# Dilated attention: two heads of a tile together, in rounds of blocks, each head in its own score bank

## What is computed

```
s = jnp.einsum('bnqrhd,bnkrhd->bnrhqk', qb, kc) * (Dh ** -0.5)
s = jnp.where(mask[None, :, None, None], s, NEG_BIG_2)
m = jnp.max(s, axis=-1, keepdims=True)
p = jnp.exp(s - m)
den = jnp.sum(p, axis=-1, keepdims=True)
o = jnp.einsum('bnrhqk,bnkrhd->bnqrhd', (p / den), vc)
lse = (m + jnp.log(den))[..., 0]
```

## Time and profile before

| | us |
|---|---|
| median of 3 runs | 3933.51 |
| profiled execution | 3931.43 |
| its span | 3930.1 |
| PE busy | 3568.4 |
| DVE busy | 1358.0 |
| POOL busy | 1278.8 |
| ACT busy | 1130.7 |

### The profile page before, as it was taken

How to read it: one execution, slowest core, us unless ns; L and a number is a source line. 1 busy time by engine, 2 the same in 40 slices (tenths; PEclk the granted TensorE clock), 3 DMA queues, 4 the chain that set the end, 5 groups by cost and what they waited for, 6 DMA issues and landing times.

```text
span 3930.1 us, 37316 instructions
## 1 busy us (share of the span) xinstructions
PE 3568.4 (91%) x15666; PEld 2807.9 (71%) x15666; DVE 1358.0 (35%) x2169; ACT 1130.7 (29%) x1545; POOL 1278.8 (33%) x335
## 2 busy tenths in 40 slices
PE   6887899998967999999996799989999889969998
PEld 5654588886734788888875688868888666647887
DVE  4337541323166422221228521242212332463123
ACT  2234332322144322322222322222222222223222
POOL 4210044442200344444433444444444420014442
PEclk9987799999977999999998899999999987769999
DMA  3110023332200233333331233324333220012332
GB/s 114 60 50 1 22 91 103 93 90 65 65 18 1 75 97 97 97 89 94 102 91 54 65 95 99 91 91 145 102 97 93 79 89 27 1 38 77 95 101 71
DMA packets 462184, 296.78 MB, mean 76 GB/s; under 512 B 14330, under 2 KB 454192, under 8 KB 462016
## 3 DMA queue, kind: packets, MB, share of 16 engines
q1 hardware_dynamic: 453664, 277.09, 24.3%
q10 hardware_dynamic: 8352, 17.30, 1.3%
HBM read 285.97 MB, written 8.39 MB: 75 GB/s over the span
## 4 chain that ended last, share of the span: by engine, by line
PE 82%; DVE 13%; ACT 3%; issue 1%; POOL 0%; DMA 0%; SPq 0%; ACTq 0%; DVEq 0%
PE bank L472 23%; PE bank L473 23%; PE bank L474 23%; PE bank L313 12%; DVE ta L733 1%; DVE xl L745 1%; DVE x L735 1%; DVE ta L1107 1%; DVE ta L512 1%; PE bank L1858 0%; POOL wlo L412 0%; DVE u L1391 0%; DVE scr L1632 0%; DVE ta L1888 0%; DVE tiny L1380 0%
## 5 line engine op out<-in xcount | busy, mean ns | idle before, releaser
L412 POOL TENSOR_TENSOR wlo<-raw,whi 128x2048 fp32r<-128x2048 f32 (+3 forms) x288 | 1210.3, 4203 | 2514.2 <-ACT whi L405 2514.2
L472 PE MATMUL bank<-xh,whi 128*128 128x512 f32 x2432 | 976.2, 401 | 70.1 <-DVE xl L745 54.4
L473 PE MATMUL bank<-xl,whi 128*128 128x512 f32 x2432 | 960.7, 395 | 0.0
L474 PE MATMUL bank<-xh,wlo 128*128 128x512 f32 x2432 | 960.4, 395 | 0.0
L405 ACT ACTIVATE whi<-raw 128x2048 fp32r<-128x2048 f32 (+3 forms) x288 | 503.4, 1748 | 712.3 <-PE bank L474 677.3
L472 PEld LDWEIGHTS bank<-xh,whi 128*128 128x128 f32 x2432 | 465.6, 191 | 198.7 <-DVE xl L745 49.3
L474 PEld LDWEIGHTS bank<-xh,wlo 128*128 128x128 f32 x2432 | 464.8, 191 | 99.6
L473 PEld LDWEIGHTS bank<-xl,whi 128*128 128x128 f32 x2432 | 465.7, 191 | 93.0
L472 PE MATMUL bank<-ah,whi 128*128 128x512 f32 x1216 | 473.0, 389 | 0.0
L473 PE MATMUL bank<-al,whi 128*128 128x512 f32 x1216 | 473.0, 389 | 0.0
L474 PE MATMUL bank<-ah,wlo 128*128 128x512 f32 x1216 | 473.0, 389 | 0.0
(11 more groups left out here) (333 smaller groups left out, 3331.6 us busy)
## 6 DMA issues: line engine op xcount, KB each, us to landing
raw<-in_ffn_w_gate SPq DMA_DIRECT2D x88, 512.0 KB, 4.0
raw<-in_ffn_w_up SPq DMA_DIRECT2D x88, 512.0 KB, 5.2
raw<-in_w_up SPq DMA_DIRECT2D x64, 512.0 KB, 4.8
raw<-in_w_down SPq DMA_DIRECT2D x64, 512.0 KB, 4.9
raw<-in_w_in SPq DMA_DIRECT2D x56, 512.0 KB, 4.7
raw<-in_ffn_w_down SPq DMA_DIRECT2D x64, 384.0 KB, 3.9
raw<-in_ffn_w_down SPq DMA_DIRECT2D x64, 320.0 KB, 3.5
raw<-in_w_out SPq DMA_DIRECT2D x16, 512.0 KB, 4.0
```

The costliest lines, as they stand in the source:

```text
L412: g.e.tensor_tensor(self.wlo[slot][:, 0:n], self.raw[slot][:, 0:n], self.whi[slot][:, 0:n].bitcast(F32), ALU.subtract).then_inc(self.lo_ma ...
L472: pe.e.matmul(bank, hi[:, at:at + P], xh, start=k == ks[0], stop=False)
L473: pe.e.matmul(bank, hi[:, at:at + P], xl, start=False, stop=False)
L474: last = pe.e.matmul(bank, lo[:, at:at + P], xh, start=False, stop=k == ks[-1])
```

## The change

PE, DVE and ACT take both heads of a tile in each step. `pairs(g)` with its places in two banks is replaced by `rounds(g)`: group 0 has two rounds, of three and of four pairs, groups 1 and 2 have one of four. In a round head 0 uses the first score bank and head 1 the second. PE issues all score products of the round, heads alternating, and then all masks, heads alternating. Head 0's weights are transposed into the transpose bank, head 1's into its own score bank after its exps. The output products of a round alternate between the heads as well; in group 0 those of the first round stand behind the scores of the second. There are 8 `yield`s to an item in groups 1 and 2, and 13 in group 0.

```diff
--- before.py
+++ after.py
@@ -1778,23 +1778,12 @@
             return self.ta[1][:], self.tb[1][:], spare(10), [wide(self.spare[:, k:k + 2, :]) for k in (11, 13)], (4, 5, 6, 7), stats
         return self.ta[0][:], self.tb[0][:], s(8), [wide(self.scr[:, k:k + 2, :]) for k in (0, 2)], (0, 1, 2, 3), stats
 
-    def pairs(self, g):
-
-        if g == 0:
-            pairs = [(0, 0, CAUSAL)] + [x for b in range(1, NB) for x in ((b, b - 1, PAST), (b, b, CAUSAL))]
-        else:
-            pairs = [(b, b, CAUSAL if g == 1 else CAUSAL4) for b in range(NB)]
-        spots, col = [], 0
-        for n in range(len(pairs)):
-            if g == 0 and n == 3:
-                col = T
-            spots.append((col // T, col % T))
-            col += P
-        spans = []
-        for qb in range(NB):
-            mine = [n for n in range(len(pairs)) if pairs[n][0] == qb]
-            spans.append((*spots[mine[0]], P * len(mine)))
-        return pairs, spots, spans
+    def rounds(self, g):
+
+        if g:
+            return [([(b, b, CAUSAL if g == 1 else CAUSAL4) for b in range(NB)], [(b, b * P, P) for b in range(NB)])]
+        meet = lambda b: [(b, b - 1, PAST), (b, b, CAUSAL)]
+        return [([(0, 0, CAUSAL)] + meet(1), [(0, 0, P), (1, P, 2 * P)]), (meet(2) + meet(3), [(2, 0, 2 * P), (3, 2 * P, 2 * P)])]
 
     def dilated_block(self, g):
         return (lambda t, b: t[:, b * P:b * P + P]) if g == 0 else (lambda t, b: t[:, b::4])
@@ -1813,9 +1802,9 @@
                 yield
             q, k, val = [self.qkv[:, 12 * m + 4 * g + i, :] for m in range(3)]
             block = self.dilated_block(g)
-            pairs, spots, spans = self.pairs(g)
+            rounds = self.rounds(g)
             if old:
-                pe.wait_ge(a, a["turned", *old, 1, (len(self.pairs(old[1])[0]) - 1) // 4])
+                pe.wait_ge(a, a["turned", *old, len(self.rounds(old[1])) - 1, 1])
             pe.wait_ge(self.tile_read, self.tile_read[first + 2 * g + i // 2])
             pair = self.reloaded[2 * g + i // 2]
             pe.wait_ge(pair, pair["all"])
@@ -1827,46 +1816,44 @@
             yield
             yield
 
-            def scores(e):
-                part = slice(e * HD, e * HD + HD)
+            def out(r):
+                pe.wait_ge(a, a["turned", *it, r, 1])
+                if old and r == 0:
+                    pe.wait_ge(v, v["out", *old])
+                at = 4 * r
+                for m, (qb, kb, mask) in enumerate(rounds[r][0]):
+                    for e in range(2):
+                        part = slice(e * HD, e * HD + HD)
+                        last = self.mm(o_bank[part, qb * P:qb * P + P], vt[:, kb * P + e * HD:kb * P + e * HD + HD],
+                                       p_bufs[e][:, (at + m) * P:(at + m) * P + P], r == 0 and m == 0, qb == NB - 1 and kb == NB - 1)
+                last.then_inc(done.tick("out", *it, r), 1)
+            for r, (pairs, spans) in enumerate(rounds):
                 pe.wait_ge(v, v["turned", *it])
-                if e:
-                    pe.wait_ge(a, a["exps", *it, 0])
+                if r:
+                    pe.wait_ge(a, a["turned", *it, r - 1, 1])
                 for m, (qb, kb, mask) in enumerate(pairs):
-                    bank, at = spots[m]
-                    dst = s_banks[bank][:, at:at + P]
-                    self.mm(dst, block(q, qb)[part], block(k, kb)[part], at == 0, False)
-                    last = self.mm(dst, self.ident16(), self.mask16(mask), False, m == len(pairs) - 1)
-                last.then_inc(done.tick("scores", *it, e), 1)
-            scores(0)
-            yield
-            for e in range(2):
-                part, p = slice(e * HD, e * HD + HD), p_bufs[e]
-                yield
-                yield
-                if e == 0:
-                    scores(1)
-                    yield
-                for r, first_pair in enumerate(range(0, len(pairs), 4)):
-                    pe.wait_ge(a, a["exps", *it, e])
-                    if r:
-                        pe.wait_ge(a, a["turned", *it, e, r - 1])
-                    elif e:
-                        pe.wait_ge(a, a["turned", *it, 0, (len(pairs) - 1) // 4])
-                    for c in range(min(4, len(pairs) - first_pair)):
-                        at = (first_pair + c) * P
-                        last = pe.e.transpose(turn_bank[:, c * P:c * P + P], p[:, at:at + P], self.c(C_IDENT))
-                    last.then_inc(done.tick("turned", *it, e, r), 1)
-                    yield
-                    yield
-                pe.wait_ge(a, a["turned", *it, e, r])
-                if old and e == 0:
-                    pe.wait_ge(v, v["out", *old])
+                    for e in range(2):
+                        part = slice(e * HD, e * HD + HD)
+                        self.mm(s_banks[e][:, m * P:m * P + P], block(q, qb)[part], block(k, kb)[part], m == 0, False)
                 for m, (qb, kb, mask) in enumerate(pairs):
-                    last = self.mm(o_bank[part, qb * P:qb * P + P], vt[:, kb * P + e * HD:kb * P + e * HD + HD],
-                                   p[:, m * P:m * P + P], m == 0, m == len(pairs) - 1)
-                last.then_inc(done.tick("out", *it, e), 1)
-                yield
+                    for e in range(2):
+                        last = self.mm(s_banks[e][:, m * P:m * P + P], self.ident16(), self.mask16(mask), False, m == len(pairs) - 1)
+                last.then_inc(done.tick("scores", *it, r), 1)
+                if r:
+                    out(r - 1)
+                yield
+                yield
+                yield
+                for e, bank in enumerate((turn_bank, s_banks[1])):
+                    pe.wait_ge(a, a["exps", *it, r, e])
+                    for m in range(len(pairs)):
+                        at = (4 * r + m) * P
+                        last = pe.e.transpose(bank[:, m * P:m * P + P], p_bufs[e][:, at:at + P], self.c(C_IDENT))
+                    last.then_inc(done.tick("turned", *it, r, e), 1)
+                yield
+                yield
+            out(len(rounds) - 1)
+            yield
             old = it
 
     def dve_dilated(self, n):
@@ -1892,22 +1878,19 @@
                 if m == 0:
                     v.wait_ge(done, done.n)
             yield
-            yield
-            for e in range(2):
-                h = 2 * i + e
-                v.wait_ge(pe, pe["scores", *it, e])
-                for qb, (bank, at, w) in enumerate(spans):
-                    last = v.e.tensor_reduce(stats[:, 0, g, qb, h:h + 1], s_banks[bank][:, at:at + w], AX.X, ALU.max, negate=True)
-                last.then_inc(done.tick("tops", *it, e), 1)
-                yield
-                yield
-                if e == 0:
-                    yield
-                for _ in range(0, len(pairs), 4):
-                    yield
-                    yield
-                yield
-            v.wait_ge(pe, pe["out", *it, 1])
+            for r, (pairs, spans) in enumerate(self.rounds(g)):
+                yield
+                v.wait_ge(pe, pe["scores", *it, r])
+                for e, bank in enumerate(s_banks):
+                    for qb, at, w in spans:
+                        last = v.e.tensor_reduce(stats[:, 0, g, qb, 2 * i + e:2 * i + e + 1], bank[:, at:at + w], AX.X, ALU.max, negate=True)
+                    last.then_inc(done.tick("tops", *it, r, e), 1)
+                yield
+                yield
+                yield
+                yield
+            yield
+            v.wait_ge(pe, pe["out", *it, len(self.rounds(g)) - 1])
             if g == 0:
                 v.e.tensor_copy(q, o_bank[:]).then_inc(done.tick("out", *it), 1)
             else:
@@ -1927,35 +1910,30 @@
             i, g = it = self.items.pop(0)
             while self.unit <= first + 2 * g + i // 2:
                 yield
-            pairs, spots, spans = self.pairs(g)
             yield
             a.wait_ge(pe, pe["tokens", *it])
             if old:
-                a.wait_ge(pe, pe["out", *old, 1])
+                a.wait_ge(pe, pe["out", *old, len(self.rounds(old[1])) - 1])
             a.e.activation(vt, turn_bank[:], ACT.Copy).then_inc(done.tick("tokens", *it), 1)
             yield
-            yield
-            for e in range(2):
-                h, p = 2 * i + e, p_bufs[e]
-                yield
-                a.wait_ge(v, v["tops", *it, e])
-                col = 0
-                for qb, (bank, at, w) in enumerate(spans):
-                    last = a.e.activation(p[:, col:col + w], s_banks[bank][:, at:at + w], ACT.Exp,
-                                          bias=stats[:, 0, g, qb, h:h + 1], accum_out=stats[:, 1, g, qb, h:h + 1])
-                    col += w
-                last.then_inc(done.tick("exps", *it, e), 1)
-                yield
-                if e == 0:
-                    yield
-                for r, first_pair in enumerate(range(0, len(pairs), 4)):
-                    m = min(4, len(pairs) - first_pair)
```

(44 more changed lines are left out.)

## The result

The changed kernel takes 3842.11 us (median of 4 runs, 3838.74 to 3845.2), the one before in the same comparison 3934.89: a ratio of 0.9763 (95% interval 0.9749 to 0.9777), 92.8 us less. Forecast were 3846.5 us and a range of 3836 to 3875. The profiled execution took 3845.2 us, its span 3843.9.

The account below looks back on a forecast made before the run. PE's own instructions plus one DVE passage per period were taken as the bound. Gains of 77 us alone and 10 shared took profiled 3931.43 to 3844.4 us; with 2.1 for the median, 3846.5, range 3836 to 3875.

Parts of the forecast that it names:

- The sum: Dilated stage: gains of 77 us alone and 10 us shared, profiled execution 3931.43 - 87 = 3844.4 us.
- Alternating products side by side: Score products on PE: both heads' records overlap; a four-block round about 1.7 us contiguous and fast, against 4.6.
- The strided form: Strided alternating scores, not in the trace: 2.7 us a round taken, to the last mask's end, against 7.3 to 7.5.
- Rival B: Strided scores: weight loads don't hide, 0.42 us per record of both heads instead of 0.21; +13.5, 3860 us; chance 0.24.
- C: Score products: order alternates but the heads take turns, scores 6.9 us instead of 2.7; 3895 us; chance 0.08.
- the two effects: Score products: alternation runs the heads' records side by side; without masks between, a weight load hides behind the product before.
- Masks: Masks grouped behind a round's products: 0.16 us for the first, 0.07 for each following; about 0.65 a strided round.
- The period: One item of the part alone: 9.75 us all fast, 11.3 all slow, the middle 10.5 taken, where it was 17.05.
- rival D: Tail wholly at PE's slow clock and 7 us of q products at double price: +7 and +7, 3860 us; chance 0.05.
- The shared part: Stage beside the q products: cheaper first-group items, less 1.5 us for stalls; gain 9.8, say 10 us.
- The outputs: Output products alternate and overlap: both heads of four blocks 1.1 us fast and 2.1 slow, where 1.9 and 3.8.
- The steps: Order of PE, DVE and ACT: steps between yields per item fall from 14 to 8 and from 18 to 13.

## Why the prediction came out right, and where it didn't

- **The time.** The sum gave 3844.4 for a profiled execution that took 3845.2. That closeness is luck: two errors of 7 us cancel in it. The medians, 87 us forecast and 92.8 measured, show the distance better. The stage gained 94 us, not 87 (75.4 alone, 18.7 shared; forecast 77 and 10). And the profiled execution lost 7 us before the stage began (3183.1 instead of 3176.1), most of it (5.5) in one place that the change doesn't touch: four operations of the norm on DVE, here with POOL's beside them, in the kernel before and after:

```profile
2629.49 4.63 POOL L412 TENSOR_TENSOR wlo<-raw,whi 128x2048 fp32r<-128x2048 f32 x1 [0.32 <-ACT whi L405]
2632.92 1.88 DVE L512 TENSOR_SCALAR ta<-const,tiny 128x128 f32<-128x128 f32 x4
```

```profile
2632.56 8.97 POOL L412 TENSOR_TENSOR wlo<-raw,whi 128x2048 fp32r<-128x2048 f32 x2 [0.40 <-ACT whi L405]
2634.60 7.41 DVE L512 TENSOR_SCALAR ta<-const,tiny 128x128 f32<-128x128 f32 x4
```

  Each long operation of DVE ends 0.09 us after one of POOL's (2634.21 behind 2634.12 before; 2637.17 and 2641.62 behind 2637.08 and 2641.53 after), so what it costs depends on where POOL's happen to lie. A 4.5 us one stands in this place in eight of the twelve profiled executions.

- **Alternating products side by side**: right. The strided form, which the trace did not have, took 2.18 us for 16 records to the masks, forecast 2.0. (The recorded sum of a strided round, 1.66 + 0.34 + 0.65, is 2.65 and not the 2.5 written; the chain went by 2.7. So too 7.05 is 7.11, and the chance of faster adds up to 0.98. None of it moves the forecast by more than a microsecond.) Rival B (0.42 a record pair) and C are out; the records of both heads start 0.01 us apart and advance 0.235. By head it is 3.31 us and not the 4.36 of two heads in turn, since half of each head's records overlap the other's even then.
- **What makes it cheap.** The step that was put wrongly is the weight of the two effects. I named alternation first and the masks' move beside it. They overlap: scores of a strided item cost 7.74 us with neither, 4.27 with masks last alone, 4.15 to 4.28 with alternation alone, 3.15 with both; the kernels 3921.3, 3857.9, 3862.7 and 3842.1 us (the first has outputs by head too: in the changed kernel that costs 2.7 us, at the slow clock of this one 0.9 us an item). Either alone brings some 50 to 60 us, the second another 16 to 20. In the kernel before, moving the masks alone brings 50.
- **The Trainium skill's rule** (TensorE: Matmul & The Clock Gate, Part 3: Packing small matmuls) that loads overlap running products only for another row group is against the measurement here: records of one head 0.11 us apart in the kernel before with masks last, where the load and the product one after the other cost 0.21.
- **Masks**: 0.65 us a round forecast, 0.97 measured at the slow clock, 0.55 at the fast. The term was too small by 0.3 us an item.
- **The period**: 10.5 forecast, 10.35 measured, but by another chain. I had scores 2.7, tops 1.8, copy 1.06, rotary 4.1. It was scores 3.15, outputs 1.9, copy 1.08, rotary 4.1 and handovers 0.1: the outputs, which I had put beside the tops and earlier, end 0.2 us after them. With scores 0.45 longer, that lifted my fast value of 9.75 to 10.35, and the slow one of 11.3 never came. So 10.5, the middle of the two, is near by luck: it was to stand for a mix of periods that DVE and that PE bound, and what it met was six much alike, with masks and outputs at the slow clock: in two (10.6 and 10.5 us) the chain goes over the partner products, in four (10.4 to 10.3) over the output copy.
- **The slow clock as rival D** did not come: the part alone has 0.81, more than the 0.69 before, though masks and outputs of most items had the slow one.
- **The shared part**: 18.7 us instead of 9.8. The price of an item was right (scores 1.19 and 1.64 us, outputs 0.80 and 1.03). What failed is that I left the q products at their old time. Their 74 chunks in this part took 60.4 us before, with stretches at the slow clock, and 54.7 after. (Both summed from start to start over what lies between the item's groups.) That is 5.7 us; the stalls I had taken off (1.5) did not come, and 1.7 is left for items a little cheaper than reckoned.
- **The outputs**: side by side, as forecast, but of little use: undone, +2.7 us, which the intervals don't tell from nothing. By head half of them overlap as well, and the clock was faster there.
- **The steps**: right in kind. They put other work between dependent parts (25 us when undone alone), but with PE's parts at the old length only 13.

What stays open: why PE had the slow clock for all the outputs in the changed kernel and only for part of them with outputs by head, and what lets the second head's records in beside the fifth of the first. The rows show that it is so, not the cause.

## What to carry to other kernels

Keep products that share a form together: a mask product of another form between f32 products costs its own switch and also stops the next weight load from hiding, and moving it alone gave 50 of the 93 us. Heads of 64 rows alternating in two banks then run side by side in full: strided scores go from 3.31 to 2.18 us a round, which gave 16 us here. When a part gets shorter, look at what is next on the chain in issue order: here the next item's partner products and rotary, behind outputs that nobody needed yet, were worth another 9 us, and with masks first 19.

## What was not expected of the hardware

- One head's 64-row records, with nothing between, start 0.11 us apart, contiguous; with a mask between, 0.21. Strided, they start 0.235 us apart, and with a mask between, 0.42.
- Two heads issued one after the other overlap by half: the second's first four records run beside the first's last four, in scores (3.31 us for sixteen strided) and in outputs (2.81 at the slow clock).
- A round of 16 strided records costs 1.1 us more than a contiguous one at the fast clock (2.18 at a granted clock of 1.00 against 1.09 to the masks), and about what contiguous ones cost at the slow clock (2.25 here and 2.08 in rows 7, to the end of the last).
- One group of four small DVE operations took 7.41 us in one execution and 1.88 in another, in code that was the same; the long ones end 0.09 us behind POOL's operations.
